# Eight operand buffers of a two-block transformer kernel moved to chosen places modulo 512 bytes

## The reference, cut to what matters

```
first block:   h = x + 0.5 * swiglu(rmsnorm(x))                       # 1024 -> 2*2816 -> 1024
               u = rmsnorm(h) @ w_mix_in                              # 1024 -> 3592
               h = h + concat(short_conv(u), gated_delta_rule(u)) @ w_mix_out
               h = h + 0.5 * swiglu(rmsnorm(h));  out = rmsnorm(h)
second block:  6 modulation vectors = silu(c) @ w_ada + b_ada         # 1024 -> 6144
               z = modulated norm @ w_in                              # 1024 -> 4800
               y_a = silu(layernorm(causal conv of 31 taps over 1024 channels)) @ w_conv_out
               y_b = attention of 8 heads (128 + 64 rotary) @ w_attn_out
               x = x + gate1 * rmsnorm((g_a*y_a + g_b*y_b) @ w_out)
               x = x + gate2 * rmsnorm(relu(h @ w_mlp_in)**2 @ w_mlp_out)   # 1024 -> 4096 -> 1024
```

## Time and profile before

| what | value |
|---|---|
| median of 3 runs | 1024.08 us (1023.53 to 1026.0) |
| the profiled execution's own time | 1023.69 us |
| its span, first to last instruction | 1021.9 us |
| TensorE matmul busy | 1005.5 us (98%), 7777 matmuls |
| TensorE weight load busy | 962.6 us (94%) |
| VectorE / ScalarE / GpSimd busy | 802.7 us (79%) / 502.8 us (49%) / 504.9 us (49%) |
| HBM read | 186.58 MB, 184 GB/s over the span |

### The profile page before, as it was taken

The page is one execution under the profiler, slowest core; times in us unless marked ns, Lnnn a source line. Parts: engine busy times, 40 slices in busy tenths (PEclk is TensorE's granted clock), DMA queues, the critical chain, the costliest instruction groups (busy, mean ns, idle before and its releaser), DMA issues.

```text
span 1021.9 us, 19068 instructions
## 1 busy us (share of the span) xinstructions
PE 1005.5 (98%) x7777; PEld 962.6 (94%) x7777; DVE 802.7 (79%) x801; ACT 502.8 (49%) x590; POOL 504.9 (49%) x294
## 2 busy tenths in 40 slices
PE   9999999999999999999999999999989999999997
PEld 7999999998999999999999999998989979999996
DVE  5788767799985579878877859998988787768764
ACT  6343433477532464434343756667567454343432
POOL 4576757510033017657677789998940104314400
PEclk9999999999999999999999999999999999999999
DMA  8968677656240267576777365582236527675641
GB/s 265 333 208 273 217 256 237 207 143 188 87 162 1 83 207 237 189 266 218 243 250 246 90 214 166 122 245 83 84 101 222 172 62 236 229 235 185 218 152 42
DMA packets 165997, 188.33 MB, mean 184 GB/s; under 512 B 10574, under 2 KB 155548, under 8 KB 165820
## 3 DMA queue, kind: packets, MB, share of 16 engines
q1 hardware_dynamic: 165580, 186.13, 56.7%
q0 software_dynamic: 192, 1.36, 0.5%
q10 hardware_dynamic: 176, 0.15, 0.1%
HBM read 186.58 MB, written 1.05 MB: 184 GB/s over the span
## 4 chain that ended last, share of the span: by engine, by line
PE 88%; POOL 4%; DVE 4%; ACT 2%; issue 1%; DMA 0%; ACTq 0%; DVEq 0%; POOLq 0%
PE ps L2006 55%; PE ps L2050 11%; PE ps L2058 9%; PE ps L2283 2%; POOL work L768 2%; PE ps L2229 2%; POOL con L765 2%; PE ps L2416 1%; PE ps L2154 1%; PE ps L2098 1%; ACT wh L799 1%; DVE wl L1291 1%; POOL work L761 1%; PE ps L2017 1%; PE ps L2430 1%
## 5 line engine op out<-in xcount | busy, mean ns | idle before, releaser
L2006 PE MATMUL ps<-xh,wh 128*128 128x256 f32 x1208 | 345.6, 286 | 2.6 <-DVE xl L1640 0.9
L2006 PE MATMUL ps<-xl,wh 128*128 128x256 f32 x1208 | 341.8, 283 | 0.0
L2006 PE MATMUL ps<-xh,wl 128*128 128x256 f32 x1208 | 341.7, 283 | 0.0
L1296 DVE TENSOR_TENSOR wl<-raw,wh 128x2048 fp32r<-128x2048 f32 x78 | 244.1, 3129 | 54.0 <-ACT wh L805 54.0
L2006 PEld LDWEIGHTS ps<-xh,wh 128*128 128x128 f32 x1208 | 231.1, 191 | 7.0 <-issue 5.0
L2006 PEld LDWEIGHTS ps<-xl,wh 128*128 128x128 f32 x1208 | 231.3, 191 | 0.5
L2006 PEld LDWEIGHTS ps<-xh,wl 128*128 128x128 f32 x1208 | 231.2, 191 | 0.0
L805 ACT ACTIVATE wh<-raw 128x2048 fp32r<-128x2048 f32 x78 | 149.0, 1911 | 141.4 <-PE ps L2006 141.4
L1291 DVE TENSOR_TENSOR wl<-raw,wh 128x2048 fp32r<-128x2048 f32 (+1 forms) x72 | 177.0, 2465 | 33.9 <-ACT wh L799 33.2
L659 POOL TENSOR_TENSOR ada_raw<-ada_raw,c_act 128x2048 f32<-128x2048 f32 x24 | 90.3, 3764 | 209.8 <-DMA ada_raw<-in_w_ada 204.7
L799 ACT ACTIVATE wh<-raw 128x2048 fp32r<-128x2048 f32 (+1 forms) x74 | 138.9, 1882 | 65.6 <-PE ps L2006 51.8
(11 more groups left out here) (415 smaller groups left out, 1859.2 us busy)
## 6 DMA issues: line engine op xcount, KB each, us to landing
raw<-in_ffn_w_in SPq DMA_DIRECT2D x43, 1024.0 KB, 7.3
ada_raw<-in_w_ada SPq DMA_DIRECT2D x24, 1024.0 KB, 5.0
raw<-in_ffn_w_out SPq DMA_DIRECT2D x22, 1024.0 KB, 4.9
raw<-in_w_in SPq DMA_DIRECT2D x18, 1024.0 KB, 5.4
raw<-in_w_mlp_in SPq DMA_DIRECT2D x16, 1024.0 KB, 5.6
raw<-in_w_mlp_out SPq DMA_DIRECT2D x16, 1024.0 KB, 4.9
raw<-in_w_mix_in SPq DMA_DIRECT2D x14, 1024.0 KB, 5.3
raw<-in_w_mix_out SPq DMA_DIRECT2D x4, 1024.0 KB, 5.2
```

What stands on the lines that cost most here:

```text
L1296: dve.tensor_tensor(wl[:, s % SLOTS, :], raw[:, s % SLOTS, :], wh[:, s % SLOTS, :].bitcast(F32), ALU.subtract).then_inc(low_done, 1)
L2006: mm = pe.matmul(bank[:, m * T:(m + 1) * T], w[:, k, m * P:(m + 1) * P], r[:, k, :], start=(m == 0 and k == 0 and j == 0), stop=(k == KT - ...
```

## The change

Before a buffer whose name stands in `HOMES` is allocated, `sb` now allocates a filler, so that the buffer begins at the given place modulo 512. `next_byte` follows the allocator's position by arithmetic.

```diff
+TURN = 512
+HOMES = {"wh": 0, "wl": 0, "xh": 128, "xl": 192, "fh": 384, "fl": 448, "yh": 256, "yl": 320}
+FIRST_BYTE = 16512
...
+        next_byte = [FIRST_BYTE]
+
         def sb(name, shape, dt=F32, where=ctx):
+            if name in HOMES:
+                fill = (HOMES[name] - next_byte[0]) % TURN
+                if fill:
+                    next_byte[0] += fill
+                    where.enter_context(nc.sbuf_tensor("before_" + name, [P, fill // 4], F32))
+            next_byte[0] += math.prod(shape[1:]) * (2 if dt == BF16 else 4)
             return where.enter_context(nc.sbuf_tensor(name, shape, dt))
...
+        work_byte = next_byte[0]
         with ExitStack() as first:
             work1 = sb("work1", [P, 17600], where=first)
+        next_byte[0] = work_byte
         yh = sb("yh", [P, KT, T], F32R)
```

## The result

The median of the kernel before is 1024.51 us (1023.53 to 1026.0), that of the changed kernel 1034.22 us (1033.25 to 1034.66), four runs each; ratio 1.0092, 95% interval 1.0075 to 1.0110. The forecast was 1009.6. The profiled execution took 1033.9 us. Its span is 1032.1 us, against 1021.9 before: 10.2 us more. The work is the same, 7777 matmuls, and TensorE is still what the end waits for.

A forecast was written before the change was run, and what follows sets the result against it. TensorE's matmul pace was taken to bound the kernel, except GpSimd between 590 and 748 us. Gains of 13.2 (x) and 2.8 us (y), less 1.5 for waits, gave 1009.6 us; range 988 to 1030 us.

The forecast's parts named there:

- the room: One ffn1 step of 17.42 us: TensorE could become 2.4 us (14%) faster before VectorE, busy 14.99 us, is next.
- Part 1, x: x matmuls move from distance 0 to 128 and 192: 3061 go from 120.0 to 115.7 ns, gaining 13.2 us.
- the two f levels: Paces of f's matmuls at distance 448 before the change: 113.8 ns in ffn1, 117.7 ns in ffn2.
- the sum: Gains of 13.2 and 2.8 make 16.0 us, less 1.5 us for delta-rule waits; forecast 1009.6 us.
- Part 2, y: y matmuls move from distance 64 to 256 and 320: 1391 go to 115.7 ns, gaining 2.8 us.
- Part 3, f: f matmuls in both swiglu parts move from 448 to 384 and 448: no change; ends 1.9 us loss, 3.7 gain.
- Part 4: Last feed-forward part, 512-column matmuls: no change taken, 1.8 us allowed either way.
- Part 5: Casts, differences, convolution and DMAs on moved buffers: no effect, covered by slack except on GpSimd between 590 and 748 us.
- The rule: TensorE's two independent read ports make operand distance worth nothing; time stays at 1024.1 us.
- The third: Rival for x, y and f: alternating high and low distances cost 122 ns, 18.1 us together, 1042.2 us; chance 0.18.
- The second rival: Distance modulo 512 does not set the pace; nothing changes or levels swap by chance: 1024.1 us within 3; chance 0.20.

The follow-up runs named there:

- experiment 8: Kernel with every distance 448, its modulation issuing three one-column matmuls per step instead of two: 1017.29 us.
- experiment 9: GpSimd's modulation multiply cut to 2 of 8 parts: every distance 448 with three one-column matmuls, 1008.37 us; changed kernel, 1033.97 us.
- experiment 10: Changed kernel with each low part at its high part's distance (x 128, y 256, f 384), so no alternation: 1028.52 us, ratio 1.0051.

## Why the prediction was wrong

**What bounds the kernel.** Right on TensorE, and that distance matters: versions that differ in nothing else span 1016.1 to 1034.2 us. Wrong on the room. "TensorE can become 2.4 us (14%) faster there before VectorE is next" looked at busy shares only. The earlier trace rows show GpSimd busy for 12.22 of 17.42 us, and I did not ask what it did in the other 5.2: it waited for a transfer that its own sum had to release. That closed round takes 17.4 to 17.8 us, so the feed-forward steps, at 17.41 us, had little left to give. I had counted 6.0 us there (10 x 96 x 4.3 ns in ffn1, 10 x 96 x 2.0 ns in ffn2); the faster version of experiment 8 lost 5.7 us to that round. In the changed kernel itself the round played no part (experiment 9).

**Part 1, x.** The step that failed is "I take the middle of the two f levels, 115.7 ns, since 128 and 192 are farther from 0 than either". It takes the pace to fall as distance grows. The runs show no such slope: the period is 256 bytes, 128 is not farther from trouble than 64, and no constant 128 goes under 118.5. It also takes one pace for one layout. The same x stood at 121.1 ns in ffn1, at 120.0 in the run of 576 and at 117.8 in the run of 240. For that last run I had expected 27.8 us and forbidden more than 28.3; it took 28.27, just inside the bound, from the wrong reason. Of the 13.2 us that the sum gives to x nothing came: ffn1 lost 1.2 us by x, the mixer gained 0.3.

**Part 2, y.** Same step, same failure: 256 is 0 again in this period. y went to 120 ns in ffn2 and stayed at 117.8 for the keys, against 115.7: a loss of 1.7 us in ffn2 for a gain of 2.8 in the sum.

**Part 3, f.** "I take no change", with a loss of 1.9 us as the worst end. It lost 5.0, the largest single term: both parts went to 121 ns. I knew that one distance had two paces and widened the range for it, but took both known paces for the whole menu; the pair of distances brought slower ones, which the tables have as 120.9 and 121.4.

**Part 4.** No change was taken, with 1.8 us allowed; it lost 1.5.

**Part 5.** Right, but the changed kernel hardly tests it: the run of 576 kept its pace, and so TensorE's two waits behind the convolution stayed (against the earlier trace rows). Every distance 448 tests it: x ran at 113.3 ns in that run, and from its first matmul to the 48 that wait for the norm it took 180.3 us against 180.6.

```profile
PE ps L2019 <- DVE work L1824: 1.7, 1, 1.7
PE ps L2540 <- DVE work L1813: 1.6, 1, 1.6
```

They were to grow by 4 us, which needed a faster x. The clock's 2.8 us were in no term. No run tests the 1.5 us that the sum takes off for waits in the delta rule's stretch.

**The rule.** The rows of 113.8 to 120.0 ns already spoke against the Trainium skill, TensorE: Matmul & The Clock Gate, section "Step-by-step: what each phase is for", by which loading the next weights takes no read bandwidth from the running matmul. For these float32r matmuls the runs bear it out still less: nothing but the two operands' distance and the start changes, and the pace goes from 113.3 to 121.4 ns. That the two reads meet is my reading of this; no run shows what happens inside.

**The rivals.** The third had the mechanism: alternation costs more than it saves, with f at the head. What was off is its picture that the pace "never settles" at 122 ns everywhere. It settles, into a pattern that repeats, at 121 ns in ffn1, about 120 for y in ffn2 and 117.8 in the mixer; so 1042.2 us was too much. And by experiment 10 it has a little over half of the feed-forward parts' loss. I gave it 0.18 because "within a run of x the weights alternate too and the pace is flat"; but the high and low weights lie at one place modulo 512, so that was no evidence on alternating distances. The second rival's remark that levels may "change places by chance" holds for the choice among a layout's patterns, not for which ones it has.

## What to carry to other kernels

Where the pace of one matmul form differs between stretches, measure that form by itself over places and over starts before moving buffers; two levels in a trace are samples, not the ends. Where operands alternate in one product, keep them at one distance from the weights, or measure the pair: two of the three pairs here were slower than their distances alone, others were not. And before an engine's speed-up is counted, follow each closed round of transfer, work and release beside it to its full length, idle time included.

## What the runs showed of the hardware that I had not expected

- Float32r matmuls of 256 columns with a load of 128 each settle into repeating patterns of 113.3 to 121.4 ns. Which are open goes with the distance of the operands, alike at four pairs 256 bytes apart; which is taken goes with the start, though starts that looked alike took different ones. Runs of up to 576 matmuls kept theirs.
- One more one-column matmul ahead of the steps raised those at 113.3 ns from 3 to 15 of 20, and to 18 once GpSimd's round was short.
- Distance 112 ran at 113.3 ns by itself and at 118.7 in the kernel, at two absolute places. Not explained.
- The best version that computes everything is every distance 448, 1016.1 us (with the added one-column matmul 1017.3, which is the same within the runs' spread). Giving the modulation weights a second buffer, so that the faster start pays as well, was not tried; with the room that the buffers leave it would have to take another's place.
